# A two-block transformer kernel on one core: the first stage in another order, gathered experts' down products in three passes, and adaLN sums twice as dense

## The reference

```python
def hier_moe(h, w_rg, b_rg, w_re, b_re, w_up, w_down):
    ...
    for n in range(N_EXPERTS):                      # 32 = 4 groups of 8
        a, b = jnp.split(h @ w_up[n], 2, axis=-1)
        out = out + combine[:, n:n + 1] * ((jax.nn.silu(a) * b) @ w_down[n])

def first_block(...):
    h = rmsnorm(x, g_mix[l])
    proj = jnp.einsum('bsd,dc->bsc', h, w_in[l])
    q_a, k_a, v_a, q_i, k_i, w_i, conv_in, q_m, gate_logits = jnp.split(proj, split_points, axis=-1)
    q_a, k_a = rope(rmsnorm(q_a)), rope(rmsnorm(k_a))      # q_i, k_i alike
    o_a = dsa_attention(q_a, k_a, v_a, q_i, k_i, w_i, topk)  # keys chosen by index scores
    o_b = conformer_conv(conv_in, conv_w[l], conv_b[l], ln_g[l], ln_b[l])
    o_m = memory_attention(q_m, mem, g_mem[l], w_mem_kv[l], g_qm[l], g_km[l])
    gates = jax.nn.sigmoid(gate_logits + b_gate[l])
    merged = gates_0 * (o_a @ w_br_a) + gates_1 * (o_b @ w_br_b) + gates_2 * (o_m @ w_br_m)
    x = x + merged @ w_o[l]
    x = x + hier_moe(rmsnorm(x, g_ffn[l]), ...)

def second_block(...):
    c_act = jax.nn.silu(c)
    for l in range(2):
        mod = (c_act @ w_ada[l] + b_ada[l]).reshape(B, 9, D_MODEL)
        ...
        h = h + 0.5 * (1.0 + gt1) * swiglu(hn, w_ffn1_in[l], w_ffn1_out[l])
        h = h + (1.0 + gt2) * (mixer(hn) @ w_mix_out[l])
        h = h + 0.5 * (1.0 + gt3) * swiglu(hn, w_ffn2_in[l], w_ffn2_out[l])
```

## Time and profile before

| | us |
|---|---|
| median of 3 runs | 1899.25 (1898.12 to 1901.4) |
| the profiled execution | 1907.31 |
| its span | 1905.5 |
| PE busy | 1853.0 (97%) |
| DVE busy | 1166.6 (61%) |
| ACT busy | 775.0 (41%) |
| POOL busy | 0.2 |

### The profile page before, as it was taken

One profiled execution on the slowest core, in us unless ns is written; L12 is line 12 of the kernel. 1 busy time (PEld: TensorE's weight loads), 2 busy tenths in 40 slices (PEclk: granted clock), 3 DMA queues, 4 the chain that ended last, 5 costly groups with the idle time before them and its releaser, 6 DMA issues.

```text
span 1905.5 us, 29853 instructions
## 1 busy us (share of the span) xinstructions
PE 1853.0 (97%) x12440; PEld 1666.4 (87%) x12440; DVE 1166.6 (61%) x1774; ACT 775.0 (41%) x1078; POOL 0.2 (0%) x4
## 2 busy tenths in 40 slices
PE   9999989899999999999999999999999999989999
PEld 8889879688866667999988889999999997879999
DVE  3594445666666646877647448776876547545443
ACT  2324533444444445343443234444444444325432
POOL 0000000000000000000000000000000000000000
PEclk9999999899999999999999999999999999999999
DMA  7334310566799976777440057876676341033451
GB/s 311 132 133 155 133 66 1 221 241 255 300 391 364 390 317 257 307 305 283 194 139 23 23 199 262 325 307 267 266 301 260 156 155 45 8 148 121 191 199 67
DMA packets 65222, 391.59 MB, mean 206 GB/s; under 512 B 7360, under 2 KB 7488, under 8 KB 27328
## 3 DMA queue, kind: packets, MB, share of 16 engines
q1 hardware_dynamic: 64800, 389.61, 53.0%
q10 hardware_dynamic: 288, 0.08, 0.0%
HBM read 388.61 MB, written 1.05 MB: 204 GB/s over the span
## 4 chain that ended last, share of the span: by engine, by line
PE 89%; DVE 6%; ACT 3%; DMA 1%; issue 1%; SPq 0%; DVEq 0%; ACTq 0%
PE bank L510 87%; PE bank L551 1%; DMA slab<-in_w_up 1%; ACT w_hi L1442 1%; DMA slab<-in_w_ffn_in 1%; DVE slab_low L1886 0%; DVE region L1950 0%; DVE tiny L1931 0%; DVE region L2479 0%; DVE region L2456 0%; DVE region L2477 0%; DVE hT L1871 0%; ACT rsB L1365 0%; DVE region L1930 0%; DVE slab_low L1967 0%
## 5 line engine op out<-in xcount | busy, mean ns | idle before, releaser
L1886 DVE TENSOR_TENSOR slab_low<-slab,w_hi 128x2048 fp32r<-128x2048 f32 x152 | 348.1, 2291 | 207.0 <-ACT w_hi L1442 206.8
L510 PE MATMUL bank<-h_hi,w_hi 128*128 128x256 f32 x1408 | 394.9, 280 | 1.5 <-DVE h_lo L1878 1.5
L510 PE MATMUL bank<-h_lo,w_hi 128*128 128x256 f32 x1408 | 396.0, 281 | 0.0
L510 PE MATMUL bank<-h_hi,slab_low 128*128 128x256 f32 x1408 | 394.9, 280 | 0.0
L1442 ACT ACTIVATE w_hi<-slab 128x2048 fp32r<-128x2048 f32 x152 | 291.1, 1916 | 163.3 <-DMA slab<-in_w_up 80.7
L510 PEld LDWEIGHTS bank<-h_hi,slab_low 128*128 128x128 f32 x1408 | 268.8, 191 | 0.0
L510 PEld LDWEIGHTS bank<-h_hi,w_hi 128*128 128x128 f32 x1408 | 264.7, 188 | 3.0 <-issue 3.0
L510 PEld LDWEIGHTS bank<-h_lo,w_hi 128*128 128x128 f32 x1408 | 264.6, 188 | 0.0
L510 PE MATMUL bank<-gT_hi,d_hi 128*128 128x256 f32 x832 | 233.8, 281 | 0.8 <-DVE gT_lo L2083 0.8
L510 PE MATMUL bank<-gT_lo,d_hi 128*128 128x256 f32 x832 | 233.7, 281 | 0.0
L510 PE MATMUL bank<-gT_hi,d_low 128*128 128x256 f32 x832 | 233.7, 281 | 0.0
(11 more groups left out here) (279 smaller groups left out, 2752.6 us busy)
## 6 DMA issues: line engine op xcount, KB each, us to landing
slab<-in_w_ffn_in SPq DMA_DIRECT2D x88, 1024.0 KB, 8.5
slab<-in_w_up SPq DMA_DIRECT2D x64, 1024.0 KB, 9.2
region<-in_w_ada SPq DMA_DIRECT2D x112, 512.0 KB, 6.6
region<-in_w_ffn_out SPq DMA_DIRECT2D x44, 1024.0 KB, 4.8
region<-in_w_down SPq DMA_DIRECT2D x32, 1024.0 KB, 5.7
slab<-in_w_in SPq DMA_DIRECT2D x23, 1024.0 KB, 4.8
slab<-in_w_mix_in SPq DMA_DIRECT2D x20, 1024.0 KB, 8.6
hT<-in_w_ada SPq DMA_DIRECT2D x32, 512.0 KB, 5.9
```

Source lines behind the costliest of these rows:

```text
L510: return nc.tensor.matmul(o, lhsT, rhs, start=start, stop=True, skip_group_check=True)
L1886: V_.tensor_tensor(slab_low[slot][:, :], slab[slot][:, :], w_hi[h % 3][:, :].bitcast(F), ALU.subtract)\
```

## The change

Eight edits, in the program's order:

1. The opening runs 4 instead of 10 warming products (`keep_warm`).
2. Stage 1: the conv blocks come first, then `qa`, then `qm`. The square sums of attention queries and keys move from b = 6 to b = 13, the rope sums from b = 8 to b = 15, the key copies into the memory keys. DVE now does the index scores and best keys of both token blocks first, then the taps, with the scalings before taps 13 to 15 and the ropes before taps 17 to 19; the memory scalings move behind the taps.
3. 4 instead of 10 gate blocks are plain; six more are split.
4. Attention: `probabilities` of the group before stands ahead of `scaled`.
5. At the joints PE waits for the high parts only (`high`), does the two products that need just those, and then waits for the low part.
6. Few experts' down products take three fp32r passes: 12 matmuls of 512 columns instead of 4 in f32. ACT makes `d_hi` at the end of each few slot, DVE a `gT_lo`, GpSimd `d_low`.
7. The `permT` copies move to other storage.
8. `ada_slot` gives the experts' segment two pieces a slot, so all 32 fall in slots 1 to 16. The places and the waits stay as they are (rate 1).

```diff
-GATES_PLAIN = 10
+GATES_PLAIN = 4
...
-    return [p for p in range(n) if 1 + p // rate == r]
+    return [p for p in range(n) if 1 + p // (rate if seg else 2) == r]
...
+                pe.wait_ge(S["dlo_few"], unit.u - PER_GROUP + 1)
+                pe.wait_ge(S["gt_lo"], low_steps(unit.steps[-1]))
...
-                        m = mm(bank[2 + half][:, :], gT_few[b][:, j, :], rows_[:, j, half * 512:(half + 1) * 512],
-                               unit.x == 0 and j == 0)
+                        o, cols = bank[2 + half][:, :], slice(half * 512, (half + 1) * 512)
+                        mm(o, gT_hi[b][:, j, 0:P], hi[:, j, cols], unit.x == 0 and j == 0)
+                        mm(o, gT_hi[b][:, j, 0:P], lo[:, j, cols])
+                        m = mm(o, gT_lo[b][:, j, 0:P], hi[:, j, cols])
...
                         for kc in range(KD):
+                            pe.wait_ge(S["h_high"], w("h_high"))
+                            for x in range(2):
+                                ffn_mm(unit, x, s + x, kc, ("high",))
                             pe.wait_ge(S["h_split"], w("h_split"))
                             for x in range(2):
-                                m = ffn_mm(unit, x, s + x, kc)
+                                m = ffn_mm(unit, x, s + x, kc, ("low",))
...
-            keep_warm(10, zeros[:, 0:P], zeros)
+            keep_warm(4, zeros[:, 0:P], zeros)
...
-            queries, early = projection(hT, 4, "act"), projection(hT, 12, "act")
+            conv, queries, memory = (projection(hT, n, "act") for n in (8, 4, 4))
...
-                if b == 6:
+                if b == 13:
                     pe.wait_ge(S["qka_sq"], w("qka_sq"))
...
-                if b == 8:
+                if b == 15:
                     pe.wait_ge(S["qka_normed"], w("qka_normed"))
...
                     if unit is not None and s == unit.steps[-1]:
                         up_high(unit.halves[1] + 2)
+                    if unit is not None and unit.kind == "few":
+                        down_high(unit)
...
+SCALES_AT, ROPES_AT = (13, 14, 15), (17, 18, 19)
+            for t in range(NT):
+                for g in range(len(GROUPS)):
+                    if GROUPS[g][0] == t:
+                        index_score(g)
+                best_keys(t)
...
+                if 1 <= i <= len(both):
+                    (_, probabilities), g = both[i - 1]
+                    probabilities(g)
                 if i < len(both):
                     (scaled, _), g = both[i]
                     scaled(g)
-                if 1 <= i <= len(both):
-                    (_, probabilities), g = both[i - 1]
-                    probabilities(g)
...
+            for unit in UNITS:
+                if unit.kind == "few":
+                    b = unit.u % 2
+                    pool.wait_ge(S["dhi_ready"], unit.u + 1)
+                    nc.gpsimd.tensor_tensor(d_low[b][:, :], d_raw[b], d_hi[d_hi_of(unit)][:, :].bitcast(F),
+                                            ALU.subtract).then_inc(S["dlo_few"], 1)
```

More of the change, by code:

```diff
@@ L119 @@
     "att_pT": "transposed probabilities", "oa_ready": "sparse attention output", "om_ready": "memory attention output",
-    "swa_ready": "window attention output", "ob_ready": "conv branch output", "ob_gate": "its sigmoid", "router_exp": "the router's exponentials",
+    "swa_ready": "window attention output", "ob_ready": "conv branch output", "ob_gate": "its sigmoid", "memh_used": "memory keys and values are projected", "router_exp": "the router's exponentials",
     "silu_ready": "silu of a gate block", "praw_ready": "RWKV projections", "lora_in": "low-rank inputs",
@@ L133 @@
     "ulo_ready": "the low part of half of a unit's up weights", "dlo_ready": "that of its down weights",
+    "dlo_few": "that of a gathered expert's down weights, by GpSimd",
     "gt_lo": "a step's turned activations, low part", "hg_low": "a chunk of the gathered h, low part",
@@ L464, in low_steps, with low_by_dve @@
         def low_steps(s):
-            return sum(len([x for x in u.steps if x <= s]) for u in UNITS if u.split)
-        def split_units(u):
-            return sum(1 for x in UNITS[:u + 1] if x.split)
+            return s + 1
+        def low_by_dve(u):
+            return sum(1 for x in UNITS[:u + 1] if x.kind != "few")
         def unit_of(s):
@@ L487, in d_hi_of @@
         def d_hi_of(unit):
-            return 0 if unit.seg == 0 else unit.u % 2
+            return 0 if unit.kind == "full" else (unit.u + 1) % 2
         block = ctx.enter_context(nc.Block())
@@ L603, in projection_split, with project_split @@
                 return block
-            def project_split(blocks, w_hi, x_hi, x_lo, paced=None, consumer="act"):
+            def project_split(blocks, w_hi, x_hi, x_lo, paced=None, high=None, consumer="act"):
                 for b in blocks:
@@ L726, in up_mm, with ffn_mm @@
                 return mm(o, a_lo, hi)
-            def ffn_mm(unit, j, s, kc):
+            def ffn_mm(unit, j, s, kc, parts=("high", "low")):
                 h = unit.halves[j]
-                if kc == 0:
+                if kc == 0 and "high" in parts:
                     pe.wait_ge(S["ulo_ready"], h + 1)
@@ L837, in down @@
             def down(unit, middle=None):
-                if unit.split:
+                if unit.kind != "few":
                     down_split(unit, unit.steps[0] == SLOTS_OF[unit.seg][0][2], middle,
@@ L983, in _ @@
                     pair_sum(B1["ka"], "rot", "dve")
-                if b == 12:
+                conv(b) if b < 8 else queries(b - 8) if b < 12 else memory(b - 12)
+            for i in range(KD):
+                pe.wait_ge(S["memh"], w("memh"))
+            keys = projection(B1["memh"], 4, "act")
+            for b in range(4):
+                if b == 2:
                     pe.wait_ge(S["ka_roped"], w("ka_roped"))
@@ L987, in _ @@
                         pair_sum(B1["ka"], f"dup{x}")
[L988 to L991 removed]
+                keys(b)
             vslab = [arrive().rearrange("p (k c) -> p k c", k=KD) for _ in range(2)]
@@ L1447, in down_high @@
                 act.wait_ge(S[f"d_in{b}"], 16 * (unit.u // 2 + 1))
-                k = unit.u - (1 if unit.seg == 0 else 2)
+                k = unit.u - (1 if unit.kind == "full" else 2)
                 if k >= 0:
@@ L1512, in moe @@
                         up_high(unit.halves[0] + 2)
-                        if unit is not members[0] and UNITS[unit.u - 1].split:
+                        if unit is not members[0] and UNITS[unit.u - 1].kind == "full":
                             down_high(UNITS[unit.u - 1])
@@ L1626, in _ @@
                 evac(B1["vm"][:, t, :], 512)
+            act.wait_ge(S["read_by_act"], w.n["read_by_act"])
+            act.sem_inc(S["memh_used"], 1)
+            for k in range(2):
+                split_slab(gate_hi, k)
             for x in range(4):
@@ L2025, in turned_low @@
                     unit = unit_of(s)
-                    if not unit.split:
-                        return
                     b, t = unit.u % 2, s - unit.steps[0]
@@ L2677, in _ @@
             w = Seen()
-            low_slabs = iter(low_used)
-            def split_slabs(n, w_hi):
-                for k in range(n):
-                    slot, _ = next(low_slabs)
-                    pool.wait_ge(S["phi_ready"], w("phi_ready"))
-                    nc.gpsimd.tensor_tensor(slab_low[slot][:, :], slab[slot][:, :], w_hi[k % 3][:, :].bitcast(F),
-                                            ALU.subtract).then_inc(S["plo_ready"], 1)
+            for unit in UNITS:
[4 more added lines that the diff above has]
+                                            ALU.subtract).then_inc(S["dlo_few"], 1)
 INPUTS = ["x", "mem", "w_in", "w_mem_kv", "w_br_a", "w_br_b", "w_br_m", "w_o", "w_up", "w_down", "c_2", "w_ada_2",
```

142 lines of the change are left out of this document (71 added, 71 removed).

## The result

The changed kernel takes 1973.95 us (median of 4 runs, 1970.5 to 1974.65) against 1900.33 for the kernel before in the same comparison: a ratio of 1.037 with an interval of 1.035 to 1.039. The forecast was 1932 with a range of 1908 to 1960. The sign and the mechanism of the largest term held.

The account below looks back on a forecast made before the run. PE was taken to bound the kernel (busy 97% of the span, 89% of the chain). Terms -2.4 -3.4 +5.2 -9.5 -2 -13 +58 = +33 on 1899.25 gave 1932 us, own range 1914 to 1942, overall 1908 to 1960.

Parts of the forecast that it names:

- the largest term: Experts' full units: up slabs queued behind adaLN pieces come late and PE waits, +58 us (43 to 63).
- The loop in the full units: Experts' full units: late slabs delay `gT_lo`, PE and DVE each round; +43 us at full clock, +15 for half clock.
- landed after 5.4: Full units: up slabs land 5.4 us after SP issues them (at most 5.6 or 6.8 by two earlier pairs).
- The first round, +8.7: Full units, from slot 3: the first delay costs +8.7 us at full clock, against +5.8 for each of six units.
- The few units: Experts' few units: down products in three fp32r passes with GpSimd's subtraction hidden, -13 us (-15 to +20).
- the rival: Few units: GpSimd's and DVE's subtractions follow one another, slot 9.2 us or more; 1949 us, to 1960; chance 0.38.
- The exclusion: Few units: GpSimd and DVE exclude each other, turning the gain of 13 us into about +4; chance 0.38.
- it is hidden if it runs undisturbed: Few units: GpSimd's subtraction, about 4.2 us, fits the some 7 us before the next slot's down product.
- Stage 1's order: Stage 1, ahead of block 15: PE waits 3.2 to 3.5 us for DVE, then half clock; +5.2 us (0 to 7).
- Attention and gates: Six more split gate blocks, -3.4 us; attention's waits for probabilities and the half clock behind them go, -9.5 us.
- The opening: Kernel's start: six fewer warming products save 2.4 us, between 1.5 and 4.2.
- Behind the experts: Joints at the mixer, output product and FFN starts: high parts first fill PE's waits for low parts, -2 us (-4 to 0).

Follow-up runs that it names:

- the two narrowed kernels: Changed kernel with up slabs issued ahead of adaLN pieces, and only 16 columns subtracted by GpSimd in one, by DVE in few units in the other: 1878.0 and 1880.6 us.

## Why the prediction was right and wrong

**The loop in the full units: right mechanism, undersized.** The forecast named the wait, its place (second slots), its releaser (`gT_lo`), that it comes seven times, and the half clock behind it; all are in the trace, and moving the slabs ahead takes 80 us away. The term was given as +58 (43 to 63) and measured +79.9, 22 more. Two steps of its sum failed, the slabs' landing time in all seven rounds (about 10 us) and an eighth round that it left out (10.3):
- *"landed after 5.4".* The slabs landed 7.6 us behind their issue in the round shown (481.27 less 473.68), and between 5.7 and 7.8 in the seven rounds, 6.9 on average. The rows had one piece issued just ahead of them; now there are two, c and d, 1.15 us apart, and both are still in flight. That they delay the slabs by sharing the DMA engines is argued and not shown: no run takes it apart. The one slab that left 1.1 us behind d landed after 5.7, but those that left 0.5 behind it range from 6.2 to 7.8. The six rounds from slot 3's turn on came to 56.4 us above the old ones, where 8.0 each, 48, was forecast; the 1.5 us of later landing in each make up that difference, while the clock's share was sized well (2.4 in the round shown, 2.2 taken).
- *The first round, +8.7.* With its 2.2 for the clock the sum gave it 10.9, and it was 12.8: its slabs landed 7.0 us behind their issue (367.49 to 374.5), again 1.6 later than taken.
- *The last round.* The sum counted "each of six units, and more in the first" and gave nothing to the round at the passage to the few units. There the down product of the last full unit stands behind the same `gT_lo`: PE waits 7.73 us and goes on at a clock of 0.58 (below), +10.3 in that slot.

```profile
569.67 0.55 PE L505 MATMUL bank<-gT_hi,d_hi 128*128 128x256 f32 x1 [7.73 <-DVE gT_lo L2041]
```

```profile
569.67:576.00 6.33, 6.33 (x33) 6.33 (x34) 6.33 (x2) 2.74 (x3) 5.59 (x1) 0.58 0.22 89
```

**The few units: the rival was right.** The forecast took GpSimd's subtraction as undisturbed (-13); the stretch measured -0.9. A slot takes 9.16 us and not 8.6, and the last down product waits another 2.2 us for GpSimd's `d_low`. The exclusion, given 0.38, is what happened, and the two narrowed kernels show it. Its own sum was off: 24 times 0.6 (9.2 less 8.6) turns -13 into +1 and not +4. By the Trainium skill's rule (SBUF — State Buffer, "Who interferes with whom") a DVE instruction with two SBUF operands and a GpSimd instruction that reads SBUF wait for each other's whole length, and here the trace agrees: 5.33 and 5.54 us in the rows above for 2.29 and 4.5. Its companion price (GPSIMD Engine Reference, section 3.1, 4497 ns) agrees too, with the 4.46 us that GpSimd took behind the end of DVE's and the 4.6 of the kernel with DVE's subtraction narrowed. From the rows 4.2 us was taken, which is near; the step that failed was "it is hidden if it runs undisturbed". I had weighed a stated rule below the absence of a row.

**Stage 1's order** cost +5.9 where +5.2 was forecast: PE waited 3.89 us (3.2 to 3.5 by the forecast) ahead of block 15 and did the sums at a clock of 0.57. **Attention and gates** came out at -13.1 against -12.9. **The opening** gave 2.9 against 2.4.

**Behind the experts** -2 became -7.3. The high-first order is worth 3.0 us alone. The rest is mostly the clock again. Two short idle stretches in the mixers, 1.36 us each in both traces, were followed by a spell at half clock before and not after, 1.7 us each. The first of them, the window of before and then that of the changed kernel:

```profile
1088.00:1091.70 3.70, 3.56 (x9) 2.87 (x10) 0.69 (x1) 0.00 (x0) 0.00 (x0) 0.54 0.02 4
```

```profile
1156.00:1159.50 3.50, 2.14 (x12) 1.81 (x10) 1.98 (x4) 0.00 (x0) 0.00 (x0) 1.00 0.02 5
```

Between the same two square sums the first mixer takes 109.6 us before, 107.9 after and 109.4 in the run with high parts first alone; the second takes 109.6, 107.9 and, in that same run, 107.9. So the order of passes does not bring it.

**The sum.** The terms were made against one profiled execution of before, 1907.31, and that one holds half-clock spells that others lack; between the traces the change is 63.2 us, between the medians 73.6. The last 10 us are a property of the two profiled executions (the one of before lies 7 above its median, the one after 3.5 below), and which share the spells have in them was not settled.

## What to carry to other kernels

Where more transfers are put into a queue that waits for consumption, look at what stands behind them: the cost is not in their bytes but in the load that can't be issued until the last of them may go, and it closes a loop whose length sets the period of the whole stretch. Sum that loop link by link with the new neighbours' transfers in it, and sum its last round by itself. GpSimd is no free help while DVE works on two operands in SBUF: lay both engines' instructions end to end in one sum.

## What the runs showed of the hardware

The same idle stretch of PE, 2.60 and 2.61 us at the same place of the program, was followed by the half clock in one execution and by the full clock in another, so a spell seen in a single profile should enter a sum with a chance and not with its whole size. A DVE subtraction of 16 columns, 0.2 us when it met nothing, lasted 1.6 to 4.4 us in about half of the cases beside GpSimd: the wait does not shrink with the width of the instruction that waits. And the piece of 1.22 us lost 4.4 us in each slot of the run with one piece a slot, where the larger subtraction in the rows of the changed kernel lost 3.0. The piece had started 0.4 us behind GpSimd's start and the subtraction 2.4 behind it: in these rows what a DVE instruction loses follows from how much of GpSimd's is still to come, not from its own size.
